# Products ahead of a data-dependent branch, and a reordered vector queue, in an expert loop on one Trainium2 core

## The reference, cut to what matters

```python
def moe_swiglu(h, w_router, b_router, w1, w3, w2):
    logits = xf @ w_router + b_router
    top_logit, top_idx = lax.top_k(logits, 2)
    top_w = jax.nn.softmax(top_logit, axis=-1)
...
    def expert_block(args):
        toks, e = args
        xb = xf[toks]
        return (jax.nn.silu(xb @ w1[e]) * (xb @ w3[e])) @ w2[e]
...
    # y[token] += top_w * its two experts' rows
x = layer_norm(DEEPNORM_ALPHA * x + (1.0 + gate) * ff, ln_ffn_g[layer], ln_ffn_b[layer])
```

## Time and profile before

| | |
|---|---|
| median of 3 runs (lowest, highest) | 1756.13 us (1749.99, 1757.92) |
| the profiled execution | 1754.97 us |
| its span in the trace | 1753.1 us |
| mean granted clock of TensorE | 0.979 |
| busy share of the span: PE, DVE, ACT, POOL | 94%, 78%, 58%, 6% |
| weights read | 496 MB through SP's queue |
| experts in the span | about 671 to 1728 us |

### The profile page before, as it was taken

The page is one execution under the profiler, slowest core; times in us unless marked ns, Lnnn a source line. Parts: engine busy times, 40 slices in busy tenths (PEclk is TensorE's granted clock), DMA queues, the critical chain, the costliest instruction groups (busy, mean ns, idle before and its releaser), DMA issues.

```text
span 1753.1 us, 20761 instructions
## 1 busy us (share of the span) xinstructions
PE 1642.9 (94%) x7272; PEld 1280.2 (73%) x7273; DVE 1362.3 (78%) x1158; ACT 1019.8 (58%) x824; POOL 107.2 (6%) x76
## 2 busy tenths in 40 slices
PE   6999899999999897999999989999899899999994
PEld 2587758888587765877887768888677677788773
DVE  5696867675796876898888986565589799888897
ACT  1375334343375343777777765445577778777672
POOL 1200010000100002002002010000100100200200
PEclk9999999999999998999999999999999999999997
DMA  9765747775565735999999986666699999999992
GB/s 365 274 246 192 267 150 268 283 266 191 200 247 184 264 113 202 380 396 361 370 351 384 395 320 219 215 219 220 240 382 396 338 389 388 364 368 352 398 394 96
DMA packets 215862, 510.47 MB, mean 291 GB/s; under 512 B 12472, under 2 KB 16744, under 8 KB 215809
## 3 DMA queue, kind: packets, MB, share of 16 engines
q1 hardware_dynamic: 208770, 496.15, 78.1%
q0 software_dynamic: 7040, 13.60, 2.2%
HBM read 510.46 MB, written 10.49 MB: 297 GB/s over the span
## 4 chain that ended last, share of the span: by engine, by line
PE 72%; DVE 10%; DMA 8%; ACT 5%; issue 4%; DVEq 0%; SPq 0%; ACTq 0%
PE ps L1575 17%; PE ps L1577 16%; PE ps L1576 16%; DMA w_raw<-in_exp_w_dram 6%; PE ps L1581 5%; PE ps L1582 5%; PE ps L1586 4%; DVE w_lo L1429 3%; ACT w_hi L841 3%; PE ps L2110 1%; PE ps L2079 1%; DVE w_lo L973 1%; DMA w_raw<-in_w_mod_mix_dram 1%; PE ps L1617 1%; DMA w_raw<-in_w_gate_dram 1%
## 5 line engine op out<-in xcount | busy, mean ns | idle before, releaser
L1429 DVE TENSOR_TENSOR w_lo<-w_raw,w_hi 128x2048 fp32r<-128x2048 f32 x332 | 757.3, 2290 | 144.7 <-ACT w_hi L841 133.1
L841 ACT CAST w_hi<-w_raw 128x2048 fp32r<-128x2048 f32 x332 | 631.6, 1912 | 164.0 <-DMA w_raw<-in_exp_w_dram 152.7
L1575 PE MATMUL ps<-w_hi,actT_hi 128*128 128x512 f32 (+1 forms) x1464 | 582.8, 398 | 41.3 <-DVE w_lo L1429 19.5
L1577 PE MATMUL ps<-w_hi,actT_lo 128*128 128x512 f32 (+1 forms) x1464 | 569.5, 389 | 0.0
L1576 PE MATMUL ps<-w_lo,actT_hi 128*128 128x512 f32 (+1 forms) x1464 | 569.1, 389 | 0.0
L1575 PEld LDWEIGHTS ps<-w_hi,actT_hi 128*128 128x128 f32 x1464 | 278.9, 191 | 113.4 <-DVE w_lo L1429 29.5
L1577 PEld LDWEIGHTS ps<-w_hi,actT_lo 128*128 128x128 f32 x1464 | 278.1, 190 | 57.8
L1576 PEld LDWEIGHTS ps<-w_lo,actT_hi 128*128 128x128 f32 x1464 | 278.8, 190 | 54.5 <-issue 1.7
L973 DVE TENSOR_TENSOR w_lo<-w_raw,w_hi 128x2048 fp32r<-128x2048 f32 x82 | 187.7, 2289 | 91.3 <-ACT w_hi L577 91.0
L577 ACT CAST w_hi<-w_raw 128x2048 fp32r<-128x2048 f32 x82 | 156.2, 1908 | 111.2 <-DMA w_raw<-in_ffn_w_dram 64.1
L1581 PE MATMUL ps<-w_hi,gT_hi 128*128 128x512 f32 x448 | 178.8, 399 | 8.3 <-DVE gT_hi L1456 6.6
(11 more groups left out here) (288 smaller groups left out, 1248.3 us busy)
## 6 DMA issues: line engine op xcount, KB each, us to landing
w_raw<-in_exp_w_dram SPq DMA_DIRECT2D x336, 1024.0 KB, 7.3
w_raw<-in_ffn_w_dram SPq DMA_DIRECT2D x33, 1024.0 KB, 5.2
w_raw<-in_w_mod_mix_dram SPq DMA_DIRECT2D x24, 1024.0 KB, 7.6
w_raw<-in_w_mod_ffn_dram SPq DMA_DIRECT2D x24, 1024.0 KB, 6.7
w_raw<-in_w_gate_dram SPq DMA_DIRECT2D x24, 1024.0 KB, 5.2
w_raw<-in_w_in_dram SPq DMA_DIRECT2D x14, 1024.0 KB, 5.4
w_raw<-in_w_out_dram SPq DMA_DIRECT2D x8, 1024.0 KB, 5.1
w_raw<-in_w_branch_c_dram SPq DMA_DIRECT2D x4, 1024.0 KB, 7.0
```

The source lines that it names most:

```text
L841: nc.scalar.copy(w_hi[:, i % SPLIT, :], w_raw[:, slot, :]).then_inc(split_hi, 1)
L1429: TTn(w_lo[:, slot, :], w_raw[:, slot, :], w_hi[:, i % SPLIT, :].bitcast(F32), ALU.subtract).then_inc(piece_used, 1)
L1575: MM(to, hi, w_h, start=first, stop=False)
L1577: return MM(to, lo, w_h, start=False, stop=last)
```

## The change

In the order of the diff: on POOL, the last LayerNorm's rows are loaded behind the last sums instead of ahead of the loop. On ACT and DVE, the outer branch of the expert is `count > HALF_P`. On DVE, the router weights are computed ahead of the wait for the positions, the selection work ahead of the wait for the gathered rows, and piece 1's low part behind it; the gate comes ahead of piece 6 in the first panel and ahead of piece 10 in the last; piece 11 comes behind the turned gates. On PE, three chunks of piece 0 (nine matmuls) stand ahead of the load of the count and of the branch. Then a one-block expert issues the fourth; a two-block expert issues the fourth, turns its second block, issues the four chunks of piece 1 for the first block, and only then waits for the second one.

```diff
@@ POOL
-                    ln_rows(I["ln_ffn_g"][1], I["ln_ffn_b"][1])
...
                         gp.sem_inc(y_home, 1)
+                    ln_rows(I["ln_ffn_g"][1], I["ln_ffn_b"][1])
                     gp.wait_ge(turned[1], EXPERTS)
@@ ACT, and the same on DVE
-                        with act.If(count > P):
-                            with act.If(count > P + HALF_P):
-                                expert(2)
+                        with act.If(count > HALF_P):
+                            with act.If(count > P):
+                                with act.If(count > P + HALF_P):
+                                    expert(2)
+                                with act.Else():
+                                    expert(2, packed=True)
                             with act.Else():
-                                expert(2, packed=True)
+                                expert(1)
                         with act.Else():
-                            with act.If(count > HALF_P):
-                                expert(1)
-                            with act.Else():
-                                expert(1, few=True)
+                            expert(1, few=True)
@@ DVE, ahead of the loop
                     TTn(gap, m2, m1, ALU.subtract).then_inc(gap_ready, 1)
                     low_h(1)
+                    dve.wait_ge(e2_ready, 1)
+                    step(TS(w2, e2, 1.0, None, ALU.add))
+                    step(nc.vector.reciprocal(w1, w2))
+                    step(TTn(w2, e2, w1, ALU.mult))
+                    TTn(tmp, is1, w1.broadcast_to(wide), ALU.mult)
+                    step(TTn(by2, is2, w2.broadcast_to(wide), ALU.mult))
+                    step(TTn(wsel[:, :, 0:EXPERTS], tmp, by2, ALU.add))
                     dve.wait_ge(pos_sent, 1)
...
-                    rest_of_piece(EXPERT, 1, sbase + MIX.n_split)
...
                     ins.then_inc(row_of_ready, 1)
-                    dve.wait_ge(gathered_lo, 1)
-                    nc.vector.tensor_copy(actT_lo[:, :, 0:P], ...
-                    rest_of_piece(EXPERT, 2, sbase + MIX.n_split)
-                    rest_of_piece(EXPERT, 3, sbase + MIX.n_split)
-
-                    dve.wait_ge(e2_ready, 1)
...
                     ins.then_inc(pick_ready, 1)
+
+                    dve.wait_ge(gathered_lo, 1)
+                    nc.vector.tensor_copy(actT_lo[:, :, 0:P], ...
+                    for i in (1, 2, 3):
+                        rest_of_piece(EXPERT, i, sbase + MIX.n_split)
@@ DVE, first panel
                             rest_at(5, done0)
+                            gate_of(3, done0, panel_0, fold_0)
                             rest_at(6, done0)
-                            gate_of(3, done0, panel_0, fold_0)
                             rest_at(7, done0)
@@ DVE, last panel
+                                if last:
+                                    gate_of(7, done, at, folds)
+                                    rest_at(10, done)
+                                    return
                                 rest_at(10, done)
                                 gate_of(7, done, at, folds)
-                                if last:
-                                    return
...
-                            rest_at(11, done6)
...
                                 gT_part(panel_0 + NP)
+                                rest_at(11, done6)
@@ PE
-                        count = pe.value_load(counts_i[0:1, bass.ds(e, 1)], min_val=0, max_val=SEQ)
...
+                        def up_chunks(multiply, i, kind, b, ks):
+                            for k in ks:
+                                ins = multiply(bank({"A": HW1, "B": HW3}[kind] + 2 * b), *chunk(k, b),
+                                               *split_piece(EXPERT, i, k % 4, 0, BANK), k == 0, k == KD - 1)
+                            return ins
+
+                        done0 = pe.snap(e * EXPERT.n + (MOD0.n_used + LAYER_PIECES + MIX.n_used))
+                        rows_ready(0)
+                        pe.wait_ge(piece_used, done0 + (1 + RING))
+                        up_chunks(product, 0, "A", 0, range(3))
+                        count = pe.value_load(counts_i[0:1, bass.ds(e, 1)], min_val=0, max_val=SEQ)
...
                             if blocks == 2:
                                 pe.wait_ge(xg_hi_ready[1], e * 2 + 2)
+                                pe.wait_ge(xg_lo_ready[1], e * 2 + 2)
+                                if packed:
+                                    pe.wait_ge(packed_ready, e + 1)
+                                for i in range(2):
+                                    up_chunks(multiply(1), i, "A", 1, range(4 * i, 4 * i + 4)).then_inc(split_used, 1)
                             else:
-                                rows_ready(0)
                                 pe.sem_inc(turned[1], 1)
-                            up(0, "A", 0, done0, second_landed)
-                            if blocks == 1:
+                                up_chunks(product, 0, "A", 0, [3]).then_inc(split_used, 1)
                                 rows_ready(1)
-                            up(1, "A", 1, done0)
+                                up(1, "A", 1, done0)
                             up(2, "B", 0, done0)
...
                         with pe.If(count > P):
+                            up_chunks(product, 0, "A", 0, [3])
+                            turn_rows(1, e + 1, TURN_LATE)
                             rows_ready(1)
-                            turn_rows(1, e + 1, TURN_LATE)
+                            pe.wait_ge(piece_used, done0 + (2 + RING))
+                            up_chunks(product, 1, "A", 0, range(4, 8))
```

More of the change, by code:

```diff
@@ L1322, in _ @@
                     number = iota[:, 0:EXPERTS].unsqueeze(1).broadcast_to(wide)
-                    logit, tmp, is1, rest, is2, sel, pos = (rt[:, n] for n in range(7))
+                    logit, tmp, is1, rest, is2, sel, pos, by2 = (rt[:, n] for n in range(8))
                     m1, i1, m2, gap, e2, w1, w2 = (rs[:, n] for n in range(7))
@@ L1402, in _ @@
                     step(TTn(w2, w2, off2, ALU.mult))
-                    dve.wait_ge(counts_ready, 1)
-                    moe_splits = LAYER_SPLITS + MIX.n_split
                     for t in range(TT):
@@ L2085, in up @@
                                 for b in range(blocks):
-                                    for k in range(4 * h, 4 * h + 4):
-                                        ins = multiply(b)(bank({"A": HW1, "B": HW3}[kind] + 2 * b), *chunk(k, b),
-                                                          *split_piece(EXPERT, i, k % 4, 0, BANK), k == 0, k == KD - 1)
+                                    ins = up_chunks(multiply(b), i, kind, b, range(4 * h, 4 * h + 4))
                                     if b == blocks - 1:
```

31 lines of the change are left out of this document (10 added, 21 removed).

## The result

The changed kernel took **1729.99 us** (median of 4 runs, 1728.66 to 1730.79) beside 1755.27 for the kernel before in the same session (4 runs, 1749.99 to 1757.92): a ratio of 0.985, 95% interval 0.983 to 0.987. It is faster, by 25 us instead of the 15 forecast, and the time lies 1 us under the range.

A forecast was written before the change was run, and what follows sets the result against it. PE, 72% of the chain, was taken as the bound, with the gains in its stops. Terms 3.9+2.2+2.0-1.0+5.0+2.0+0+3.4-2.7 = 14.8 us off 1754.97 gave 1740 us, range 1731 to 1752.

The forecast's parts named there:

- Expert 0, forecast 5.0: Expert 0's start: DVE's low parts come sooner, PE's stop before the turn shortens by 3.7 us, less half clock; bounds 2 and 7.
- part 2: DVE ahead of the loop: router weights and selection work moved into waits, so DVE reaches the loop 1.2 us sooner.
- Expert 5, forecast 0: PE's branch at expert 5's start: nine products and branch wait for the turned rows, long branch stays; bounds -2 and 3.
- rival (c): No long PE branch left: shorter loop code makes experts 4 and 5 jump fast, 13.4 instead of 2.0 us; 1729 us, chance 0.12.
- Expert 4, forecast -2.0: PE's branch at expert 4's start: nine products ahead cover part of the long branch, 2.0 us gained; bounds 0 and 4.
- Expert 3, forecast 3.4: Packed expert 3's start: products on both sides of the second block's turning shorten PE's stop, 3.4 us gained; bounds 2.5 and 4.2.
- Gates: DVE's earlier gates shorten PE's stops: 3.9 us in expert 1, 2.2 in expert 6, 2.0 at the last expert's end.
- Branches of ACT and DVE, forecast -1.0: Expert loop: 0.4 us saved once in expert 0; cold code at DVE's first middle expert costs 1.0, bounds 0 and 4.3.
- (a): The stream takes it back: PE's gains in experts 0, 4 and 7 become waits for weights; 1748 us, chance 0.20.
- (b): Cold code on DVE and ACT: middle code costs 4.3, expert 0 gains 2, row loads cost 5; 1749 us, chance 0.12.
- (d): New long PE branches: experts 1, 2, 6 and 7 stop too, 6.7 us each; 1767 us, chance 0.07.
- (e): Small experts save a fetch each time: ACT's second branch had stopped it in all five; 1734 us, chance 0.03.

The follow-up runs named there:

- Both runs of this part: DVE's old order ahead of the loop put back in the changed kernel, 1739.21 us; the new order alone on the kernel before, 1745.44 us.
- its shifted version: 32 narrow products at the program's start, shifting all later PE code: on the kernel before 1755.49 us, on the changed kernel 1732.07 us.
- the three parts tried alone: Kernel before with only DVE's new order ahead of the loop, 1745.44 us; only DVE's new gate order, 1750.05 us; only PE's part, 1752.77 us.

## Why the prediction was wrong

By the table, the 9.8 us between the 14.8 forecast and the 24.6 of the two traces are: expert 5's start 8.5 more, expert 0 3.0 more, expert 3 1.6 more, expert 7 1.0 more, expert 4 2.7 less, experts 5 to 6 and 6 to 7 0.4 and 1.2 less. The terms for experts 0 and 5 are the two that failed.

**Expert 0, forecast 5.0, measured 8.0** (-9.6 and +1.6 of start; the start alone lay between 682.9 and 685.5 in three traces of the changed kernel, between 683.9 and 684.5 in two of the one before, so the 1.6 need not be the change's). The step that failed is part 2's "DVE reaches the loop 1.2 us sooner", and with it the sum for expert 0 ("684.86-1.2-0.4+2.29"), which left the 8.59 us of issue standing but for 0.4. It counted the moved operations by their durations and asked only what they wait for. It did not ask what runs while the sequencer fetches. The sequencer left for the loop 7.8 us sooner, not 1.2. How much of its way shows as "issue" depends on the work that the engine has queued then, 0.8 us before and 8.0 after. Both runs of this part show it: 7.5 us to undo it, 11.7 us alone. The range of 2 to 7 for this term was too narrow too: its upper end kept PE's stop as the only gain, where the stop itself is longer in other executions.

**Expert 5, forecast 0, measured -8.5.** The step "branch at 1366.4, done at 1372.4" took the 6.02 us of one execution as a constant of the code. It is none. The forecast listed the case as rival (c), "No long branch left on PE", at 13.4 instead of 2.0 us for the two. Half of it came: expert 5 short, expert 4 long. Its reason, the shorter code, has nothing for it: expert 4 stayed long, and the unchanged code of before jumped both ways. Part of this gain is luck of the execution: with a long branch there the changed kernel would have taken 5.5 to 7.9 us more, some 1736 to 1738 us, inside the range. That is an estimate from the stretches above; one run of it did take 1738.31 us, without a trace.

**Expert 4, forecast -2.0, measured +0.7.** The nine products did cover 2 us, but the branch took 6.26 us instead of 3.67 (6.2 to 6.4 in the three traces of the changed kernel). It was 3.7 to 4.1 us in both traces of the kernel before and in its shifted version, and 5.2 to 6.6 in all others, those with PE's old order too, so the nine products are not the reason. This is no scatter of single executions as in expert 5: each of the three parts tried alone made the branch longer (5.8, 6.1 and 6.3 us), for a reason that stays open. The bounds of 0 and 4 missed this.

**Expert 3, forecast 3.4, measured 5.0**, inside the mechanism: the stop is 3.37 us instead of 5.42, with 12 products on each side of the turning. In this execution no half clock followed. In two further traces of the changed kernel and in the run with the row loads back it did (0.79 over 8 us, beside 1.00 here), and the stretch took 127.2 to 127.5 instead of 124.5 us: a gain of 2.0 to 2.3. The forecast lies between.

**Gates.** Right in mechanism. Expert 1 gave 2.9 (1.33 of stop and 1.7 of half clock) and expert 6 1.0, less than 3.9 and 2.2: the step "2.2 of that go" took a whole low part off the stop, of which 1.16 us stay. The end gave 2.4 us beside 2.0, from the last turn to the last matmul. That experts 3 to 5 "have none" of this stop was true only while a long branch stood in its place in expert 5.

**Row loads, forecast -2.7, measured -3.6**, as a wait of ACT for weights in expert 7. The bound was 6.6. It came ahead of the place that the forecast gave, at 1616.78 us instead of behind 1640, with the four gathers beside them.

**Branches of ACT and DVE, forecast -1.0**: nothing, in either sense. DVE did not stop at its first middle expert.

**Rivals.** (a), the stream takes it back, is out for expert 0, which kept its 9.6 us. (b) is out: DVE's longest wait at its first middle expert was 1.4 us, for ACT, though the row loads cost more than forecast. (d) is out: no branch of experts 1, 2, 6 and 7 was long in any trace, shifted or not. (e) is out: with the old nesting the sequencer's 2.2 us at the second branch, once, reached no other engine.

The rule that was weighed ahead of the forecast fares as follows. In the kernels here experts 1, 2, 6 and 7 jump in 0.2 us and the long ones, among experts 0, 4 and 5, in 3.6 to 6.8 us, in the same code and not the same ones each time. The Trainium skill, "Runtime: NRT & Kernel Launch", section "Instruction fetch mechanics", has each taken branch out of two cache lines stall. The traces agree in so far as some of these branches stand for microseconds. They disagree that each one does, if all their targets lie outside, which no trace shows: the same branch of expert 5 took 6.02 us in one execution and 0.23 in the next.

## What to carry to other kernels

Read a stop marked "issue" behind a branch as time of the sequencer that nothing covered, and look at how much work stands in the engine's queue when it leaves: put long operations that wait for nothing of their own engine last before far code, and chains of short ones that wait for each other first. Take the length of such a stop from several executions, not one, and price both cases. Where two waits overlap, as the long branch and the gate in expert 5, each alone is worth little (from expert 4's sums to 6's 2.7 us for the short branch in the kernel before, 1.1 for the gate) and both together are worth 8.1 us; an edit that removes one is judged only with the other gone.

## What was not expected of the hardware

The same far branch of PE in the same kernel took 0.2 us or 6 us from one execution to the next: expert 5's 6.02 us in one trace of the kernel before, short in another. DVE's first entry into the loop cost 8.6 to 16.6 us in kernels whose DVE code ahead of it is the same. And the same stop of 3.4 us (expert 3) was followed by half clock in two executions of the changed kernel and not in the third, which moved that stretch by 2.7 to 3.0 us.
